# Prompt attention of a two-layer decoder: 64-row score products in two halves, five score banks, two rows of lead

## The chip, the cores and the metric

The kernel runs on one core of a Trainium2 chip. TensorE (PE) multiplies into PSUM banks, VectorE (DVE) and ScalarE (ACT) evict and transform, GpSimd (POOL) is a third elementwise engine, and SyncE (SP) issues the DMAs. The metric is the device time of one launch in microseconds, the median of several runs.

## The reference

One inference step of a two-layer decoder for a prompt of 2048 rows and a sample group of 64 rows: a gated linear attention layer, then a differential attention layer. The part in question is the prompt's differential attention, with 8 heads of 128 values, each in two halves m = 0, 1 of 64:

```python
s = jnp.einsum('bqhmd,bkhmd->bhmqk', qs, ks).astype(F32) * (DIFF_DH ** -0.5)   # DIFF_DH = 64
s = s + bias[None, :, None]                       # bias by distance, constant from a distance of 128 on
s = jnp.where(rel >= 0, s, jnp.finfo(F32).min)    # causal
p = jax.nn.softmax(s, axis=-1)
a = p[:, :, 0] - lam * p[:, :, 1]
return jnp.einsum('bhqk,bkhd->bqhd', a, v.astype(F32))
```

## The kernel before

The program is a sequence of stages with a barrier between them: projection, recurrence, residual, projection, prompt attention, sample attention, residual. The change touches the prompt attention alone.

It goes over 8 heads H, and in each over 16 query rows i, a row being a tile of 128 queries against its (i+1)*128 keys. The keys of a row are cut into pieces of at most 512 columns from the right (10 at 1, 4 at 4 pieces: 40 pieces a head for each half m). A loop of three rounds covers two heads each; heads 6 and 7 stand behind it.

- **Scores** (`scores`, L1609 and L1610). Operands are split into a high and a low float32r part, so that three partial products are needed for q times k (high-high, high-low, low-high). `q_hl` holds for each half m the 64 rows of the high part of q over the 64 rows of its low part, and `k_hi`, `k_lo` hold each half's keys twice, one copy over the other. So one product over 128 rows gives two partial products at once, and a piece takes two of them, into one of four banks `ps_s`.
- **Preparation** (`prep`, `high`, `low`). The q and k of the next head are loaded (`load_nat`, 8 DMAs for each of four groups of rows), turned by TensorE four tiles at a time (L1590) into the bank `ps_k`, copied as the high part by ACT (L1680) and subtracted as the low part by DVE (L1739 for q, L1742 for k). There are 16 such steps for a head, one beside each row.
- **Eviction** (`take`, L1765 and L1773). DVE adds the bias, writes the scores of the row to `s_sb` and keeps the maximum of each piece. Behind the last piece it reduces the maxima (L1780) and negates them (L1782).
- **Exponentials** (`exps`, L1686). ACT raises both halves of the row and sums them (`total`). `take` and `exps` run one row ahead of the rest.
- **Combination** (`combine`, L1790 to L1798). DVE takes the reciprocal of the two sums, the weight of the second half, and writes `a` = first half + weight * second half.
- **Turning and values** (`turn` L1623, `copies` L1698, `meet` L1637, `output` L1705). TensorE turns `a` in groups of four tiles into two banks `ps_a`, ACT copies them to `a_t` (two buffers), TensorE multiplies them by v in full float32 (two records for each tile), ACT scales the row and SP stores it.

TensorE's order is written out by hand: for row i the preparation step, then the scores of row i+2 with the turning and the values of row i mixed in from the fourth score piece on. DVE's order in `head` is `take(i+1)`, `combine(i)`, `low`. Each engine works strictly in its own order and waits on semaphores.

## Time and profile before

| | |
|---|---|
| median of 3 runs | 4059.39 us (4054.75 to 4062.89) |
| the profiled execution | 4064.68 us, its span 4062.9 us |
| PE busy | 3668.9 us (90%), 19279 products |
| DVE busy | 1798.8 us (44%) |
| ACT busy | 1123.8 us (28%) |
| POOL busy | 118.7 us (3%) |
| mean granted TensorE clock | 0.953 of full speed |

The shares are means over all stages. The prompt attention has about 900 us of the span, from its first DMA at 2257 us to its last output at 3154 us, and it is the only long stretch in which DVE is busy for more than eight tenths of the time. A busy PE in the profile includes the tail of each product, so the spacing of starts says more than the busy time.

### The profile page before, as it was taken

The numbers are of one execution on the slowest core, as the hardware profiler recorded it, in microseconds if no ns is written. First come the engines' busy times: TensorE is split into PE (matmuls) and PEld (weight loads), VectorE is DVE, ScalarE is ACT, GpSimd is POOL, SyncE is SP. The second block draws the span as 40 slices with busy tenths as digits, with TensorE's granted clock in tenths as the row PEclk, the third lists the DMA queues.
The fourth block names the chain that finished last, engine by engine and source line by source line (L and its number), as shares of the span: only waits on it lengthen the run. The fifth ranks groups of instructions, "written<-read, shape, count | busy, mean of one in ns | idle before, by whom it ended". The sixth has DMA issues, their size and how long they took to land. (4 is left out here: it accounts for less than half of the span.)

```text
span 4062.9 us, 56102 instructions
## 1 busy us (share of the span) xinstructions
PE 3668.9 (90%) x19279; PEld 3005.8 (74%) x19279; DVE 1798.8 (44%) x4077; ACT 1123.8 (28%) x1848; POOL 118.7 (3%) x156
## 2 busy tenths in 40 slices
PE   3999997995999989999999688888888799779999
PEld 2788896774788868888888577777777677458887
DVE  2122201555555542223000588888888222165554
ACT  1111101332221221112000366666666111121111
POOL 0000001110000000000000000000000000000000
PEclk7999998998999989999999799999999899889999
DMA  5433443336222244334222622222210555242221
GB/s 141 146 125 106 142 138 119 114 105 226 74 88 83 73 164 145 108 124 146 98 98 90 132 64 64 54 52 54 64 33 12 200 200 205 104 157 85 74 85 47
DMA packets 321076, 440.41 MB, mean 108 GB/s; under 512 B 155213, under 2 KB 214382, under 8 KB 320894
## 3 DMA queue, kind: packets, MB, share of 16 engines
q1 hardware_dynamic: 320894, 438.24, 33.2%
q8 instruction: 83, 1.36, 0.1%
q14 instruction: 99, 0.81, 0.1%
HBM read 296.46 MB, written 141.70 MB: 108 GB/s over the span
## 5 line engine op out<-in xcount | busy, mean ns | idle before, releaser
L318 PE MATMUL in_ps_y<-in_w_hi,in_x_hi 128*128 128x512 f32 (+2 forms) x2040 | 771.6, 378 | 12.8 <-ACT in_w_hi L359 5.5
L320 PE MATMUL in_ps_y<-in_w_lo,in_x_hi 128*128 128x512 f32 (+2 forms) x2040 | 768.4, 377 | 0.0
L322 PE MATMUL in_ps_y<-in_w_hi,in_x_lo 128*128 128x512 f32 (+2 forms) x2040 | 768.3, 377 | 0.0
L318 PEld LDWEIGHTS in_ps_y<-in_w_hi,in_x_hi 128*128 128x128 f32 x2040 | 385.0, 189 | 76.9 <-issue 11.7
L322 PEld LDWEIGHTS in_ps_y<-in_w_hi,in_x_lo 128*128 128x128 f32 x2040 | 384.7, 189 | 64.2
L320 PEld LDWEIGHTS in_ps_y<-in_w_lo,in_x_hi 128*128 128x128 f32 x2040 | 384.9, 189 | 63.1
L1637 PE MATMUL att_ps_o<-att_v,att_a_t 128*128 128x128 f32 x2176 | 296.2, 285 | 55.3 <-ACT att_a_t L1698 54.7
L1637 PEld LDWEIGHTS att_ps_o<-att_v,att_a_t 128*128 128x128 f32 x2176 | 277.8, 197 | 80.6 <-ACT att_a_t L1698 56.8
L1765 DVE TENSOR_SCALAR_CACHE_REDUCE att_s<-att_ps_s,att_far 128x512 f32<-128x512 f32 (+3 forms) x608 | 326.7, 582 | 6.0 <-PE att_ps_s L1610 2.0
L439 DVE COPY in_out<-in_ps_y 128x512 f32<-128x512 f32 (+1 forms) x85 | 55.8, 657 | 604.8 <-PE in_ps_y L322 604.8
L1686 ACT ACTIVATE att_s<-att_s,att_neg 128x128 f32<-128x128 f32 (+15 forms) x256 | 307.1, 1200 | 2.7 <-DVE att_neg L1782 2.1
L1609 PE MATMUL att_ps_s<-att_k_hi,att_q_hl 128*128 128x512 f32 (+3 forms) x640 | 260.9, 414 | 11.7 <-DVE att_s L1765 10.8
L372 ACT ACTIVATE in_out<-in_ps_y 128x512 f32<-128x512 f32 (+1 forms) x102 | 56.3, 552 | 740.2 <-PE in_ps_y L322 663.2
L1610 PE MATMUL att_ps_s<-att_k_lo,att_q_hl 128*128 128x512 f32 (+3 forms) x640 | 235.5, 373 | 0.0
L1202 PE MATMUL res_ps_f<-res_w_hi,res_o_hi 128*128 128x512 f32 x544 | 220.7, 406 | 7.8 <-ACT res_w_hi L1314 3.9
L1202 PE MATMUL res_ps_g<-res_w_hi,res_h_hi 128*128 128x512 f32 x544 | 219.2, 403 | 3.9 <-issue 3.9
L1204 PE MATMUL res_ps_f<-res_w_lo,res_o_hi 128*128 128x512 f32 x544 | 217.3, 399 | 0.0
L1206 PE MATMUL res_ps_f<-res_w_hi,res_o_lo 128*128 128x512 f32 x544 | 216.9, 399 | 0.0
L1206 PE MATMUL res_ps_g<-res_w_hi,res_h_lo 128*128 128x512 f32 x544 | 216.5, 398 | 0.0
L1204 PE MATMUL res_ps_g<-res_w_lo,res_h_hi 128*128 128x512 f32 x544 | 216.4, 398 | 0.0
L1623 PE MATMUL att_ps_a<-ident,att_a 128*128 128x128 f32 x1088 | 162.4, 279 | 35.0 <-DVE att_a L1798 33.6
L1698 ACT ACTIVATE att_a_t<-att_ps_a 128x512 f32<-128x512 f32 (+2 forms) x320 | 159.7, 531 | 120.9 <-PE att_ps_a L1623 119.9
(242 smaller groups left out, 5078.4 us busy)
## 6 DMA issues: line engine op xcount, KB each, us to landing
smp_k_pg<-in_cache_k SPq DMA_DIRECT2D x64, 512.0 KB, 5.1
smp_v_pg<-in_cache_v SPq DMA_DIRECT2D x64, 512.0 KB
x_turned<-in_x_hi SPq DMA_DIRECT2D x34, 512.0 KB, 5.0
x_turned<-in_x_lo SPq DMA_DIRECT2D x34, 512.0 KB, 5.8
factors<-in_out SPq DMA_DIRECT2D x68, 256.0 KB, 2.0
in_x_hi<-x_turned SPq DMA_DIRECT2D x34, 512.0 KB, 4.3
in_x_lo<-x_turned SPq DMA_DIRECT2D x34, 512.0 KB, 5.1
res_factors<-factors SPq DMA_DIRECT2D x34, 512.0 KB
```

What stands on the lines that cost most here:

```text
L318: nc.tensor.matmul(ps_y[g][:, cols], x_hi[u][:, k, :], w_hi[g][:, k, cols], start=(k == 0), stop=False)
L320: nc.tensor.matmul(ps_y[g][:, cols], x_hi[u][:, k, :], w_lo[g][:, k, cols], start=False, stop=False)
L322: mm = nc.tensor.matmul(ps_y[g][:, cols], x_lo[u][:, k, :], w_hi[g][:, k, cols], start=False, stop=(k == KD - 1))
L1202: nc.tensor.matmul(dst[:, cols], hi[kind][:, k, :], w_hi[n][:, k, cols], start=(k == 0), stop=False)
L1204: nc.tensor.matmul(dst[:, cols], hi[kind][:, k, :], w_lo[n][:, k, cols], start=False, stop=False)
L1206: mm = nc.tensor.matmul(dst[:, cols], lo[kind][:, k, :], w_hi[n][:, k, cols], start=False, stop=(k == K - 1))
L1609: nc.tensor.matmul(dst, lhs, k_hi[u][m][:, lo_:hi_], start=True, stop=False)
L1610: nc.tensor.matmul(dst, lhs, k_lo[u][m][:, lo_:hi_], start=False, stop=True).then_inc(s["piece_ready"], 1)
L1623: mm = nc.tensor.transpose(ps_a[n % 2][:, (b % 4) * P:(b % 4 + 1) * P], a[i % 2][:, b * P:(b + 1) * P], core.ident[:, :])
L1637: mm = nc.tensor.matmul(ps_o[:, 0:D_VD], a_t[n % 2][:, (b % 4) * P:(b % 4 + 1) * P], v_sb[u][:, b, :], start=(b == 0), stop=(b == i))
L1686: nc.scalar.activation(s_sb[i % 2][:, m, 0:n], s_sb[i % 2][:, m, 0:n], ACT.Exp, bias=neg[i % 2][:, m:m + 1], accum_out=total[i % 2][:, m:m ...
L1765: ins = nc.vector.tensor_scalar(s_sb[i % 2][:, m, lo_:cut], ps_s[n % RING][:, 0:cut - lo_], far[u][:, :], None, ALU.add, ALU.max, accum_ou ...
```

## The change

The scores are computed with products over 64 rows. Half m lies on rows 64m to 64m+63 of `q_hi`, `q_lo`, `k_hi`, `k_lo`, each kept once, and a pair of pieces (the same keys for m = 0 and 1) takes six products: high-high, high-low, low-high, each for m = 0 on the upper 64 rows and m = 1 on the lower 64, into two banks. There are five banks `ps_s` in place of four and no `ps_k`; the preparation shares the two `ps_a`. The preparation has 8 steps for a head in place of 16 and `load_nat` 2 DMAs for each group in place of 8.

All scores are kept with the opposite sign (`HEAD_SCALE` is negative, the bias comes from `rev_neg`), so that the row's minimum is what ACT needs; it is one `tensor_reduce` right behind the row's evictions. `take` and `exps` run two rows ahead (`LAG`), TensorE's scores three rows and two pairs (`LEAD`). `s_sb` has four buffers, `a_t` eight. The reciprocal and the weight are computed on GpSimd with three small operations. The values of row i are multiplied in the iteration behind that in which it is turned.

```diff
+    HEAD_SCALE = -(D_DH ** -0.5)
+    SLOTS, ROW_RING, TURN_RING = 5, 4, 8
+    LAG, LEAD = 2, 2
...
+    prep_at = {1: 0, 3: 1, 5: 2, 7: 3, 9: 4, 11: 5, 13: 6, 14: 7}
...
-        q_hl = [[sb(f"q_hl{u}{m}", [P, SEQ], F32R) for m in range(2)] for u in range(2)]
-        s_sb = [sb(f"s{i}", [P, 2, SEQ]) for i in range(2)]
+        k_hi = [sb(f"k_hi{u}", [P, SEQ], F32R) for u in range(2)]
+        k_lo = [sb(f"k_lo{u}", [P, SEQ], F32R) for u in range(2)]
+        q_hi = [sb(f"q_hi{u}", [P, SEQ], F32R) for u in range(2)]
+        q_lo = [sb(f"q_lo{u}", [P, SEQ], F32R) for u in range(2)]
...
-        ps_k = ps("ps_k")
...
-                        for side in range(2):
-                            for m in range(2):
-                                sp.dma_start(nat[:, 4 * g:4 * g + 4, m, side, :],
-                                             src[g * BANK:(g + 1) * BANK, bass.ds(h * D_VD + m * D_DH, D_DH)]
-                                             .rearrange("(t p) d -> p t d", p=P)).then_inc(nat_in[g], 16)
+                        sp.dma_start(nat[:, 4 * g:4 * g + 4, :],
+                                     src[g * BANK:(g + 1) * BANK, bass.ds(h * D_VD, D_VD)]
+                                     .rearrange("(t p) d -> p t d", p=P)).then_inc(nat_in[g], 16)
...
+                    pe.wait_ge(s["piece_free"], after(PIECES * H + 2 * at + 2))
+                    for q_part, k_part in ((q_hi, k_hi), (q_hi, k_lo), (q_lo, k_hi)):
+                        for m in range(2):
+                            rows = slice(m * D_DH, (m + 1) * D_DH)
+                            mm = nc.tensor.matmul(ps_s[(2 * at + m) % SLOTS][:, 0:hi_ - lo_],
+                                                  q_part[u][rows, i * P:(i + 1) * P], k_part[u][rows, lo_:hi_],
+                                                  start=(q_part is q_hi and k_part is k_hi), stop=(q_part is q_lo))
+                    mm.then_inc(s["piece_ready"], 1)
...
+                    for i in range(1, T + 1):
+                        turning = [] if last and i == T else list(range(groups[i % T]))
+                        end = PAIRS if last else 2 * PAIRS
+                        row = i + LAG + 1
+                        filling = [n for n in range(first_pair(row) + LEAD, first_pair(row + 1) + LEAD) if n < end]
+                        meeting = list(range(groups[i - 1]))
+                        for step in range(max(len(turning), len(filling), len(meeting) + 1)):
+                            if step < len(turning):
+                                turn(H, u, i, step, last)
+                            if step == 0 and i in prep_at and not last:
+                                prep(H + 1, prep_at[i], bank_free(H, last, ("prep", i, prep_at[i])))
+                            if step < len(filling):
+                                scores(H, u, filling[step])
+                            if step >= 1 and step - 1 < len(meeting):
+                                meet(H, u, i - 1, step - 1)
...
+                    for i in range(1, T + 1):
+                        turning = not (last and i == T)
+                        more = not (last and i + LAG >= T)
+                        if turning:
+                            copies(H, u, i, 0, 1, last)
+                            if not last and i in prep_at:
+                                use = bank_uses(last).index(("prep", i, prep_at[i]))
+                                high(H + 1, 1 - u, prep_at[i], ps_a[use % 2])
+                        if more:
+                            exps(*ahead(H, u, i, LAG), 0)
+                        if turning:
+                            copies(H, u, i, 1, 3, last)
+                        if more:
+                            exps(*ahead(H, u, i, LAG), 1)
+                        if turning:
+                            copies(H, u, i, 3, 4, last)
+                        output(H, i - 1)
...
+                def weights(H, i):
+                    r = i % ROW_RING
+                    pool.wait_ge(s["exp_done"], after(2 * (T * H + i + 1 + ROW_RING)))
+                    nc.gpsimd.tensor_tensor(inv[r][:, :], total[r][:, :], minus_one[:, :],
+                                            ALU.pow).then_inc(s["inv_done"], 1)
+                    pool.wait_ge(s["inv_done"], after(T * H + i + 1))
+                    nc.gpsimd.tensor_tensor(ratio[:, :], total[r][:, 0:1], inv[r][:, 1:2],
+                                            ALU.mult).then_inc(s["ratio_done"], 1)
+                    pool.wait_ge(s["ratio_done"], after(T * H + i + 1))
+                    nc.gpsimd.tensor_tensor(weight[r][:, :], ratio[:, :], core.neg_lambda[:, :],
+                                            ALU.mult).then_inc(s["weight_done"], 1)
...
+                        for m in range(2):
+                            bank, at = ps_s[(2 * n + m) % SLOTS], col
                             if cut > lo_:
-                                ins = nc.vector.tensor_scalar(s_sb[i % 2][:, m, lo_:cut],
-                                                              ps_s[n % RING][:, 0:cut - lo_], far[u][:, :], None,
-                                                              ALU.add, ALU.max, accum_out=mx[:, m, col:col + 1])
-                                col += 1
+                                ins = nc.vector.tensor_scalar(s_sb[r][:, m, lo_:cut], bank[:, 0:cut - lo_],
+                                                              far[u][:, :], None, ALU.subtract, ALU.min,
+                                                              accum_out=low_of[i % 2][:, m, at:at + 1])
+                                at += 1
...
+                def lowest(H, u, i, cols):
+                    dve.wait_ge(s["piece_free"], after(PIECES * H + 2 * first_pair(i + 1) + SLOTS))
+                    dve.wait_ge(s["exp_done"], after(2 * (T * H + i + 1)))
+                    nc.vector.tensor_reduce(shift[i % ROW_RING][:, :], low_of[i % 2][:, :, 0:cols], AX.X,
+                                            ALU.min).then_inc(s["shift_done"], 1)
...
-                    dve.wait_ge(s["exp_done"], after(2 * (T * H + i + 1)))
-                    if i >= 2:
-                        dve.wait_ge(s["o_copied"], after(T * H + i - 1))
-                    nc.vector.reciprocal(inv[i % 2][:, :], total[i % 2][:, :]).then_inc(s["inv_done"], 1)
-                    dve.wait_ge(s["inv_done"], after(T * H + i + 1))
-                    nc.vector.scalar_tensor_tensor(weight[:, :], total[i % 2][:, 0:1], core.neg_lambda[:, :],
-                                                   inv[i % 2][:, 1:2], ALU.mult, ALU.mult).then_inc(s["weight_done"], 1)
...
-                        if not (last and i + 1 >= T):
-                            take(*ahead(H, u, i, 1))
+                        more = not (last and i + LAG >= T)
+                        if more:
+                            lowest(*ahead(H, u, i, LAG), take(*ahead(H, u, i, LAG)))
+                        if not last and i - 1 in prep_at:
+                            n = prep_at[i - 1]
+                            use = bank_uses(last).index(("prep", i - 1, n))
+                            low(H + 1, 1 - u, n, ps_a[use % 2])
                         combine(H, u, i)
```

## Rows read from the trace of the kernel before

**Rows 1.** Busy time by window, attention: stretch, length, PE, PEld, DVE, ACT, POOL, clock, DMA.
```profile
2257.00:2287.10 30.10, 14.04 (x72) 12.08 (x72) 13.40 (x30) 10.22 (x20) 0.00 (x0) 0.61 1.13 213
2287.10:2400.70 113.60, 96.39 (x618) 81.84 (x619) 93.75 (x313) 71.47 (x135) 0.00 (x0) 0.92 0.38 76
2400.70:2509.30 108.60, 95.88 (x646) 81.77 (x645) 93.81 (x313) 73.09 (x137) 0.00 (x0) 0.98 0.25 61
...
2951.20:3058.00 106.80, 94.91 (x635) 81.20 (x634) 92.52 (x312) 72.65 (x137) 0.00 (x0) 0.97 0.13 32
3058.00:3154.10 96.10, 85.40 (x576) 73.76 (x574) 80.41 (x282) 63.81 (x118) 0.00 (x0) 0.98 0.04 12
```

**Rows 2.** Who waited for whom, 2287 to 3154 us: total, times, longest.
```profile
ACT att_o L1705 <- DMA mixer_out<-att_o: 32.4, 7, 8.1
DVE att_q_hl L1739 <- ACT att_q_hl L1680: 27.9, 15, 6.4
DVE att_inv L1790 <- ACT att_s L1686: 25.3, 12, 3.8
DVE att_k_lo L1742 <- ACT att_k_hi L1680: 22.0, 8, 4.4
```

**Rows 3.** Groups of instructions by form, attention: count, busy us, mean ns, idle before.
```profile
L1637 PE MATMUL att_ps_o<-att_v,att_a_t 128*128 128x128 f32 x2176 | 296.2, 285 | 55.3 <-ACT att_a_t L1698 54.7
...
L1609 PE MATMUL att_ps_s<-att_k_hi,att_q_hl 128*128 128x512 f32 x448 | 197.4, 441 | 10.3 <-DVE att_s L1765 9.6
...
L1623 PE MATMUL att_ps_a<-ident,att_a 128*128 128x128 f32 x1088 | 162.4, 279 | 35.0 <-DVE att_a L1798 33.6
```

**Rows 4.** Timeline of TensorE, around row 13 of head 3: start, length, instruction.
```profile
2705.30 0.47 PE L1609 MATMUL att_ps_s<-att_k_hi,att_q_hl 128*128 128x512 f32 x1
2705.61 0.39 PE L1610 MATMUL att_ps_s<-att_k_lo,att_q_hl 128*128 128x512 f32 x1
2705.84 0.39 PE L1609 MATMUL att_ps_s<-att_k_hi,att_q_hl 128*128 128x512 f32 x1
...
2712.19 1.06 PE L1637 MATMUL att_ps_o<-att_v,att_a_t 128*128 128x128 f32 x8
2713.08 0.38 PE L1623 MATMUL att_ps_a<-ident,att_a 128*128 128x128 f32 x2
```

**Rows 5.** Timeline of TensorE in the sample attention: 8-row products among 128-row ones.
```profile
3240.97 1.07 PE L2042 MATMUL smp_ps_o<-smp_v_new,smp_a_new 8*64 8x512 f32 x2
3241.96 7.08 PE L2040 MATMUL smp_ps_o<-smp_v_pg,smp_a_t 128*64 128x512 f32 x16
3248.97 1.07 PE L2042 MATMUL smp_ps_o<-smp_v_new,smp_a_new 8*64 8x512 f32 x2
```

**Rows 6.** Timeline of DVE behind the evictions of a row and in the next, head 3.
```profile
2704.11 0.16 DVE L1780 TENSOR_REDUCE att_top<-att_mx 128x2 f32<-128x10 f32 x1
2704.31 0.17 DVE L1782 TENSOR_SCALAR att_neg<-att_top 128x2 f32<-128x2 f32 x1
...
2705.03 2.08 DVE L1798 SCALAR_TENSOR_TENSOR att_a<-att_s,att_weight 128x1792 f32<-128x1792 f32 x1
2707.15 0.69 DVE L1739 SCALAR_TENSOR_TENSOR att_q_hl<-att_ps_k,att_q_hl 64x512 fp32r<-64x512 f32 x1
...
2709.22 0.75 DVE L1765 TENSOR_SCALAR_CACHE_REDUCE att_s<-att_ps_s,att_far 128x512 f32<-128x512 f32 x1
...
2709.89 0.48 DVE L1765 TENSOR_SCALAR_CACHE_REDUCE att_s<-att_ps_s,att_far 128x256 f32<-128x256 f32 x1
```

**Rows 7.** Groups of instructions, GpSimd over the whole span.
```profile
L1338 POOL TENSOR_TENSOR res_rstd<-res_rstd,minus_half 128x1 f32<-128x1 f32 x34 | 18.7, 551 | 418.9 <-DVE res_rstd L1386 418.9
```

**Rows 8.** Timeline of the attention's start: DMA issues of SP, then DVE's first eviction.
```profile
2256.99 3.39 SPq L1537 DMA_DIRECT2D att_k_nat<-out_k  x4
...
2276.24 0.54 SPq L1542 DMA_DIRECT2D att_v<-out_v  x1
...
2284.11 0.29 DVE L1773 CUSTOM_DVE_ANT_0 att_s<-att_ps_s,att_bias 128x128 f32<-128x128 f32 x1 [0.37 <-DMA att_far<-in_rel_bias]
```

More of the change, by code:

```diff
@@ new lines, in bank_free @@
+                def bank_free(H, last, use):
+                    order = bank_uses(last)
+                    at = order.index(use)
+                    kind, i, n = order[at - 2] if at >= 2 else ("prob", 0, at - 2)
+                    if kind == "prep":
+                        pe.wait_ge(s["lo_done"], after(PREPS * (H + 1) + n + 1))
+                    else:
+                        done = GROUPS * (i // T) + first_group[i % T] + n + 1
+                        pe.wait_ge(s["a_copied"], after(GROUPS * H + done + 2))
+                    return ps_a[at % 2]
@@ new lines, in turn @@
+                def turn(H, u, i, g, last):
+                    H2, u2, i2 = ahead(H, u, i)
+                    if g == 0:
+                        pe.wait_ge(s["a_done"], after(T * H2 + i2 + 1 + ROW_RING))
+                    bank = bank_free(H, last, ("prob", i, g))
+                    for b in range(4 * g, min(4 * g + 4, i2 + 1)):
+                        mm = nc.tensor.transpose(bank[:, (b % 4) * P:(b % 4 + 1) * P],
+                                                 a[i2 % 2][:, b * P:(b + 1) * P], core.ident[:, :])
@@ L1673, in _ @@
+                pe.sem_inc(s["a_met"], TURN_RING)
+                pe.sem_inc(s["a_turned"], groups[T - 1])
+                for n in range(PREPS):
+                    prep(0, n, first_banks[n])
+                for n in range(first_pair(LAG + 1) + LEAD):
+                    scores(0, 0, n)
+                turn(0, 0, 0, 0, False)
+                for n in range(first_pair(LAG + 1) + LEAD, first_pair(LAG + 2) + LEAD):
+                    scores(0, 0, n)
                 over_heads(pe, head)
@@ L1708, in head @@
                 def head(H, u, last):
-                    for i in range(T):
-                        todo = [] if last else list(enumerate(slots(i)[0]))
-                        for n, (is_q, m, g) in todo[:1]:
-                            high(H + 1, 1 - u, slots(i)[1] + n, is_q, m, g)
-                        more = not (last and i + 1 >= T)
-                        if more:
-                            exps(*ahead(H, u, i, 1), 0)
-                        copies(H, i, 0, 2)
-                        if more:
-                            exps(*ahead(H, u, i, 1), 1)
-                        copies(H, i, 2, groups[i])
-                        output(H, i)
-                        for n, (is_q, m, g) in todo[1:]:
-                            high(H + 1, 1 - u, slots(i)[1] + n, is_q, m, g)
@@ L1777, in take @@
-                                col += 1
+                                    out=s_sb[r][:, m, start:hi_], in0=bank[:, start - lo_:hi_ - lo_],
+                                    in1=bias[u][:, NEAR - (n_keys - start):NEAR], scale=1.0, scalar=3.0e38,
+                                    op0=ALU.add, op1=ALU.min, accum_out=low_of[i % 2][:, m, at:at + 1])
+                                at += 1
                             ins.then_inc(s["piece_free"], 1)
-                    dve.wait_ge(s["piece_free"], after(PIECES * H + first_piece[i + 1] + RING))
@@ L1814, in _ @@
+                        combine(H, u, i)
+                for n in range(PREPS):
+                    low(0, 0, n, first_banks[n])
+                dve.wait_ge(s["lo_done"], after(PREPS))
+                dve.sem_inc(s["piece_free"], SLOTS)
+                dve.sem_inc(s["a_done"], ROW_RING)
+                dve.sem_inc(s["shift_done"], 2)
+                for i in range(LAG):
+                    lowest(0, 0, i, take(0, 0, i))
                 over_heads(dve, head)
```

278 lines of the change are left out of this document (124 added, 154 removed).

## The prediction

> **What bounds the kernel now.** I read the busy time by window first, because the page's shares are means over seven stages. From the first to the last instruction of the prompt attention [rows 1] there are 30 us of start, seven heads that take 110.1 us each ((3058.0 - 2287.1) / 7) and an eighth of 96.1 us. In a head DVE is busy for 93.7 us and PE's records cover about 96, but these overlap: a product of 512 columns is recorded with 0.39 us and the next one starts 0.23 us behind it [rows 4]. By spacing PE needs less. With 0.111 us for each 128-column record (0.89 us for 8, rows 4), the values take 2176 / 8 x 0.111 = 30.2 us, the turning 1088 / 8 x 0.111 = 15.1 us [rows 3], the preparation 64 x 0.111 = 7.1 us. Of the 160 score products of a head 112 are 512 wide (448 in all for each of the two lines, rows 3), 25.8 us at 0.23; the 48 narrower ones lie between 0.11 and 0.17 us by their width, some 6.5 us. Together 84.7 us, so DVE is the fuller engine.
>
> The waits say where the other 16 us of a head go. DVE waited 27.9 + 22.0 us for high parts of the preparation and 25.3 us for exponentials [rows 2], together 9.4 us a head. The cause of much of it is at the head's start, where ACT's `output` stood for a store (32.4 us in seven waits, rows 2) and everything behind it on ACT with it; at the head's end `take` of the short row 0 is done at once and `combine(15)` waits for two long exponentials. Behind row 5 DVE hardly waits: the timeline behind a row's evictions is one dependent instruction after the other [rows 6].
>
> **DVE's part.** Today 0.92 us pass from the start of the reduction to that of the combination (2704.11 to 2705.03, rows 6). The negation, the reciprocal and the weight go away; the reduction (0.16 us) stays, with some 0.05 us to the next start. This gives back 0.7 us a row, 11.2 us a head. The preparation has 8 steps fewer at 0.69 us (rows 6; the low part of q is 64x512 there, and the k part of 128 rows costs the same 0.69, so the full-height q part should too): 5.5 us. The evictions and the combination stay as they are. A subtract or a minimum in the place of an add or a maximum is not in the trace; I take the same duration, since only the operation changes. DVE's work falls from 93.7 to 77 us, 81 with the short gaps between dependent instructions.
>
> **TensorE's part.** Preparation: 32 records fewer, 3.6 us. Turning and values stay, 45.3 us. The scores go from two products a piece and half to three, so for a pair of pieces from four to six. No row here shows two 64-row products on different halves of the array. The bounds: if the two of a step run at once, a step costs what one product costs, 0.23 us at 512 columns, and for narrow pieces not less than two weight loads of 0.11 us. That is 28 pairs x 3 x 0.23 + 12 x 3 x 0.22 = 27.2 us a head, against 32.3 now. If they run one after the other it is 28 x 6 x 0.23 + 12 x 6 x 0.135 = 48.4 us. These ends are far apart. I take the lower one: the nearest row is the 128-row product [rows 4], which streams all 128 rows in the same 0.23 us, and two 64-row products together read no more rows and load no more cells.
>
> The Trainium skill supports this: TensorE: Matmul & The Clock Gate, in Part 3 on packing small matmuls, says that products on distinct row groups run concurrently, with starts some 4 ns apart. No row of this trace shows it. The other way, TensorEngine Tiling (Array Packing), Key Properties, says that a change of the tiling mode drains the engine. By that rule every pair of this kernel pays a drain on both sides, since its neighbours use all 128 rows.
>
> What a visit to another shape costs can be seen: the two 8-row products of the sample attention take 0.99 us to the next start, where two of their 128-row neighbours take 7.01 / 16 x 2 = 0.88 [rows 5], so 0.11 us a visit. The first float32r product behind float32 ones has 0.31 us to the next start, and not 0.23 [rows 4], 0.08 more. There are 40 visits a head, one a pair: 40 x 0.19 = 7.6 us. (Today's visits are fewer, as the scores often stand in runs.) PE: 45.3 + 3.5 + 27.2 + 7.6 = 83.6 us. So PE hardly gets shorter, while DVE does, and PE becomes the fuller engine by a little.
>
> **Waits and queues.** GpSimd takes the reciprocal and the weight. Its power on 128x1 took 0.55 us [rows 7]; on 128x2 I take 0.7, the two products between 0.15 and 0.55 each, so a chain of 1.0 to 1.8 us. It starts when the exponentials of row i end, and `combine(i)` comes a whole `take` and `combine` later, at least 2 us on short rows and 7 on long ones, so it is hidden; without that cover it would cost up to 1 us on rows 0 to 3. GpSimd has nothing else queued here. `lowest` adds a wait for exponentials four rows back, long past. With two rows of lead the wait for exponentials at row 15 goes too (25.3 / 8 = 3.2 us a head). At a head's start SP now issues 2 DMAs before v and the bias and not 8; at 0.54 us each (2.16 for four, and 3.39 for the first four with their start, rows 8) this is 3.2 us sooner for the stores for which ACT stood. What is late next is TensorE's third turning group at rows 9 and 11: its bank waits for the low part of a preparation step, which DVE does only behind the next `take`. At row 9 that is 13 tiles x 2 x 0.67 / 4 = 4.4 us of evictions (0.67 us for four tiles, rows 6), 0.2 of reduction and 0.7 of low part, 5.3 us behind the combination, where TensorE is there after two groups turned, the preparation, two pairs and a group of values, 2 x 0.44 + 0.44 + 2 x 0.88 + 0.89 = 4.0. Behind it are the score pairs of the next row; DVE has two pairs in hand, so I take 1 us for each.
>
> Over 83.6 us of PE I set 5 us for what doesn't overlap (these two, short rows, the loop's turn). A head: 88.5 us.
>
> **The start and the end.** v is issued at 2276.2 behind 32 DMAs, DVE's first eviction is 7.9 us later [rows 8]. Now 8 DMAs stand before it; with 8 preparation steps, each in a bank of its own, it comes some 15 us sooner, and I take 13, for two rows are to be evicted before the exponentials matter. Head 7 loses 11.2 us of DVE work and its row-15 wait: 82 us for 96.1.
>
> **Sum.** 7 x (110.1 - 88.5) = 151, and 14 and 13: 178 us. The profiled execution is 4064.7 us, 1.8 outside its span and 5 above the median of the runs; I take the 178 from the median: 4059 - 178 = 3881 us.
>
> **The rivals.**
> - *DVE sets the pace* (0.17): the visits cost nothing and PE stays under 80 us. The head is 82 us, DVE's work and gaps: 197 + 14 + 13 = 224 less, 3835 us. For it: float32 turning and values are already switched with float32r scores today. Against: rows 5.
> - *PE and DVE take turns* (0.20). Only 2.5 pairs fit in five banks, and TensorE can't turn row i before the combination. Where one engine has a long iteration, the other's is short: at row 13 DVE evicts row 15 and combines, 5.4 + 0.2 + 0.7 + 2.1 = 8.4 us, and PE has 14 tiles to turn, the one pair of row 0, 13 tiles of values and the preparation, 5.8 us; a row later DVE has 3.7 and PE 6.1. If neither can run ahead, the larger counts in each; over the 16 rows that is 92 us, with 4 for the short rows and the loop 96: 99 + 9 + 13 = 121 less, 3938 us.
> - *The halves don't overlap* (0.12): PE needs 83.6 + 21.2 = 104.8 us, with 4.5 not hidden 109.3. The heads gain 6 us in all, the start 13 and the end nothing: 4040 us.
> - *The halves exclude each other* (0.05), the one on the other side: the product on one half starts only when that on the other has left the array, so each takes its recorded 0.39 us and not 0.23 (rows 4; 0.27 for narrow ones). The scores then cost 28 x 6 x 0.39 + 12 x 6 x 0.27 = 85 us a head, PE 141, the head 146: 7 x 36 + 25 more, 4320 us. It decides from 112 us a head on, that is, if a 64-row product costs over 0.015 us more than a full one with no overlap.
> - *As forecast* (0.46): 85 to 92 us a head, 3857 to 3906 us.
>
> **Range and chances.** 3815 to 3965 us holds the first three cases, with bounds of the unknown terms, and leaves out the two without overlap. A difference of 0.2% (8 us) is about what a measurement of this kernel can tell from none. Faster 0.91 (the case without overlap mostly belongs here), within 0.2% 0.03, slower 0.06.
>
> **What would show it.** In the profile after: pairs of score records that start within a few hundredths of a microsecond, the next step 0.23 us behind; if starts are 0.23 us apart within a pair, the third rival holds. DVE busy 77 us a head. Heads of 88 us. Few waits of DVE for exponentials or high parts; a wait of TensorE for `lo_done` at rows 9 and 11. DVE's first eviction near 2270 us. The prediction is wrong if the visits cost several tenths, if the granted clock falls in the attention (it is 0.92 to 0.98 in the heads now, rows 1), or if GpSimd's chain shows up before the combination.

## The result, and the profile after

The changed kernel takes 3945.5 us (median of 4 runs, 3944.4 to 3950.6), beside 4057.1 us for the kernel before on the same chip (4051.1 to 4062.9): a ratio of 0.9728, 95% interval 0.971 to 0.9745. That is 112 us less. 178 were forecast, and 3881 us; the range, 3815 to 3965 us, holds the result. One of the four executions of the kernel with the low part inside `take` (see the experiments) fell into a slower state of the chip (4681.7 us, mean granted clock 0.733) and is left out, so its median below is that of the other three.

The page's busy times, over all stages:

```profile
span 3943.8 us, 56028 instructions
PE 3622.2 (92%) x19663; PEld 2902.4 (74%) x19663; DVE 1679.3 (43%) x3629; ACT 1080.3 (27%) x1784; POOL 277.0 (7%) x541
```

The prompt attention by windows: the start, heads 0 to 6 together, heads 0 and 1, and most of head 7. The columns are start:end, length, then busy us and instructions of PE, weight load, DVE, ACT and POOL, the granted clock, the DMA share and GB/s.

```profile
2254.70:2273.30 18.60, 10.00 (x62) 8.00 (x62) 8.38 (x27) 6.54 (x16) 1.88 (x5) 0.68 0.98 264
2273.30:2944.40 671.10, 622.27 (x4678) 475.29 (x4677) 550.64 (x1792) 465.46 (x885) 137.93 (x335) 0.99 0.16 44
2273.30:2362.10 88.80, 81.88 (x599) 60.60 (x598) 78.60 (x256) 62.99 (x117) 19.07 (x47) 0.97 0.18 48
2362.10:2459.90 97.80, 91.37 (x686) 69.89 (x684) 78.82 (x257) 67.26 (x129) 19.59 (x48) 0.98 0.16 46
2944.40:3032.40 88.00, 85.43 (x662) 67.10 (x661) 70.47 (x229) 64.22 (x121) 18.33 (x45) 1.00 0.05 14
```

Against [rows 1] the start takes 18.6 us for 30.1. Heads 0 to 6 take (2944.4 - 2273.3) / 7 = 95.9 us each for 110.1, and head 7, from 2944.4 to 3038.5, takes 94.1 for 96.1. So the gain is 11.5 + 7 x 14.2 + 2 = 113 us. The forecast was 13 + 151 + 14. DVE's work fell as expected, to 78.7 us a head, but a head did not follow it down: neither engine is busy for all of it. The mean over seven heads hides the first one, which went from 113.6 to 88.8 us; heads 1 to 6 gained 12.5 us each.

The clock has a share in this. The seven heads of the kernel before, together:

```profile
2287.10:3058.00 770.90, 672.01 (x4411) 572.69 (x4412) 655.00 (x2184) 506.72 (x951) 0.00 (x0) 0.96 0.25 59
```

The granted clock rose from 0.96 to 0.99: 770.9 x 0.04 - 671.1 x 0.01 = 24 us of the heads' 99.8 would be the clock, if all of it came through. Head 0 alone went from 0.92 to 0.97. Whether the clock rose because of the change, no run here shows.

TensorE's timeline at rows 8 and 9 of a head. Columns: start, us, line, output<-inputs, tile shapes, count; a bracket is idle time before it and what ended it.

```profile
2602.17 0.28 PE L1624 MATMUL att_ps_s<-att_k_hi,att_q_lo 64*128 64x128 f32 x2
2602.37 1.16 PE L1662 MATMUL att_ps_o<-att_v,att_a_t 128*128 128x128 f32 x8
...
2605.79 0.65 PE L1648 MATMUL att_ps_a<-ident,att_a 128*128 128x128 f32 x4
2606.28 0.60 PE L1607 MATMUL att_ps_a<-ident,att_k_nat 128*128 128x128 f32 x4
2606.81 0.50 PE L1624 MATMUL att_ps_s<-att_k_hi,att_q_hi 64*128 64x512 f32 x2
2607.14 0.39 PE L1624 MATMUL att_ps_s<-att_k_lo,att_q_hi 64*128 64x512 f32 x2
2607.37 0.40 PE L1624 MATMUL att_ps_s<-att_k_hi,att_q_lo 64*128 64x512 f32 x2
2607.70 0.66 PE L1648 MATMUL att_ps_a<-ident,att_a 128*128 128x128 f32 x4
...
2611.87 0.44 PE L1648 MATMUL att_ps_a<-ident,att_a 128*128 128x128 f32 x2 [1.53 <-DVE att_k_lo L1794]
```

The two halves run at once: two products of 512 columns take 0.23 us to the next two (2607.14 to 2607.37), as long as one full-height product does in [rows 4]. But the visit costs more than what I took for it. The four products ahead of it take 0.53 us to the first score and not 0.44; the first step takes 0.33 and the last one 0.33, where 0.23 would do. Over the 117 visits with 512 columns between 2370 and 2940 us that stand free of waits, the mean is 0.14 us ahead of the scores and 0.19 in them, 0.33 a visit.

DVE behind the row's evictions, to be read beside [rows 6]:

```profile
2603.44 0.42 DVE L1826 CUSTOM_DVE_ANT_0 att_s<-att_ps_s,att_bias 128x256 f32<-128x256 f32 x1
2603.79 0.08 DVE L1826 DVE_READ_ACCUMULATOR2_ANT att_low_of<- 128x1 f32 x1
2604.00 0.16 DVE L1839 TENSOR_REDUCE att_shift<-att_low_of 128x2 f32<-128x8 f32 x1
2604.11 1.55 DVE L1848 SCALAR_TENSOR_TENSOR att_a<-att_s,att_weight 128x1280 f32<-128x1280 f32 x1
2605.57 0.35 DVE L1819 TENSOR_SCALAR_CACHE_REDUCE att_s<-att_ps_s,att_far 128x128 f32<-128x128 f32 x1
```

From the reduction to the combination it is 0.11 us and was 0.92. The reduction ends 0.05 us behind the combination's start: nothing that DVE does next waits for it.

The waits between 2273 and 3032 us (engine, tile and line that waited, what it waited for: us in all, times, the longest), to be read beside [rows 2]:

```profile
ACT att_o L1728 <- PE att_ps_o L1662: 114.7, 100, 3.0
ACT att_a_t L1720 <- PE att_ps_a L1648: 107.1, 124, 2.8
...
DVE att_k_lo L1794 <- ACT att_k_hi L1700: 36.5, 13, 5.8
DVE att_s L1819 <- PE att_ps_s L1624: 32.3, 59, 2.2
...
DVE att_a L1848 <- POOL att_weight L1777: 27.7, 10, 3.9
DVE att_q_lo L1791 <- ACT att_q_hi L1700: 19.5, 7, 2.9
...
PE att_ps_a L1648 <- DVE att_q_lo L1791: 10.6, 7, 1.5
PE att_ps_a L1648 <- DVE att_k_lo L1794: 10.6, 7, 1.5
...
ACT att_o L1728 <- DMA mixer_out<-att_o: 3.4, 3, 1.8
```

ACT's wait for a store fell from 32.4 to 3.4 us. DVE's wait for exponentials at row 15 is gone in heads 0 to 6, but exponentials are still waited for under another name: of the ten waits for the weight (27.7 us, beside 25.3 us for exponentials in [rows 2]) seven stand at row 1 of a head, 2.6 to 3.5 us each, and in each the weight's first operation starts 0.1 us behind the row's last exponentials, 1.3 us before the combination. DVE's wait for high parts is not gone either: 36.5 + 19.5 = 56.0 us, 8 a head, where [rows 2] have 49.9. Fourteen of these waits, 32 us, belong to the preparation steps of rows 13 and 14 (some 1.8 and 2.8 us each) and six, 24 us, to that of row 1: some 3.2 us in four heads, 5.8 and 5.5 us in heads 2 and 4, with which a round of the loop begins. DVE's timeline at the beginning of head 4:

```profile
2660.43 0.48 DVE L1848 SCALAR_TENSOR_TENSOR att_a<-att_s,att_weight 128x256 f32<-128x256 f32 x1 [2.57 <-POOL att_weight L1777]
...
2669.22 0.69 DVE L1794 TENSOR_TENSOR att_k_lo<-att_ps_a,att_k_hi 128x512 fp32r<-128x512 f32 x1 [5.45 <-ACT att_k_hi L1700]
```

TensorE works without a gap from 2651 to 2665.6 there, on the values of rows 14 and 15 with the turning of rows 15 and 0 and two score pairs between them; the preparation step of row 1, whose high part DVE waits for, stands behind them in TensorE's order. In heads 2 and 4 TensorE then stands for 1.7 and 1.9 us more, and the trace names nothing that it waited for. And TensorE in its turn waits 1.5 us for a low part in front of the third turning group of rows 9 and 11.

### The profile page after: what moved, and what is told of

Same layout as the page of the kernel before. It is cut to its first block and busy times, and to the rows that moved or that the text cites. A ratio compares the mean times of both kernels' runs of the same rounds, so it can differ in the third digit from the quotient of the medians.

```text
span 3943.8 us, 56028 instructions
## 1 busy us (share of the span) xinstructions
PE 3622.2 (92%) x19663; PEld 2902.4 (74%) x19663; DVE 1679.3 (43%) x3629; ACT 1080.3 (27%) x1784; POOL 277.0 (7%) x541
## 5 line engine op out<-in xcount | busy, mean ns | idle before, releaser
L1819 DVE TENSOR_SCALAR_CACHE_REDUCE att_s<-att_ps_s,att_far 128x256 f32<-128x256 f32 (+3 forms) x608 | 331.6, 581 | 35.3 <-PE att_ps_s L1624 32.3
L1662 PEld LDWEIGHTS att_ps_o<-att_v,att_a_t 128*128 128x128 f32 x2176 | 265.5, 192 | 61.6 <-issue 50.7
L1662 PE MATMUL att_ps_o<-att_v,att_a_t 128*128 128x128 f32 x2176 | 309.8, 286 | 0.5 <-ACT att_o L1728 0.5
L1707 ACT ACTIVATE att_s<-att_s,att_shift 128x128 f32<-128x128 f32 (+15 forms) x256 | 306.3, 1198 | 3.5 <-DVE att_shift L1839 3.5
L1648 PE MATMUL att_ps_a<-ident,att_a 128*128 128x128 f32 x1088 | 181.0, 282 | 39.9 <-DVE att_a L1848 13.1
L1720 ACT ACTIVATE att_a_t<-att_ps_a 128x512 f32<-128x512 f32 (+2 forms) x320 | 169.5, 533 | 111.4 <-PE att_ps_a L1648 107.9
L1848 DVE SCALAR_TENSOR_TENSOR att_a<-att_s,att_weight 128x128 f32<-128x128 f32 (+15 forms) x128 | 172.4, 1347 | 28.5 <-POOL att_weight L1777 27.7
L1648 PEld LDWEIGHTS att_ps_a<-ident,att_a 128*128 128x128 f32 x1088 | 122.0, 142 | 81.0 <-issue 37.7
```

The costliest lines, as they stand in the source:

```text
L1648: mm = nc.tensor.transpose(bank[:, (b % 4) * P:(b % 4 + 1) * P], a[i2 % 2][:, b * P:(b + 1) * P], core.ident[:, :])
L1662: mm = nc.tensor.matmul(ps_o[:, 0:D_VD], a_t[n % TURN_RING][:, (b % 4) * P:(b % 4 + 1) * P], v_sb[u][:, b, :], start=(b == 0), stop=(b == i))
L1707: nc.scalar.activation(s_sb[r][:, m, 0:n], s_sb[r][:, m, 0:n], ACT.Exp, bias=shift[r][:, m:m + 1], scale=-1.0, accum_out=total[r][:, m:m + ...
L1720: nc.scalar.activation(a_t[n % TURN_RING][:, 0:cols], bank[:, 0:cols], ACT.Copy).then_inc(s["a_copied"], 1)
L1819: ins = nc.vector.tensor_scalar(s_sb[r][:, m, lo_:cut], bank[:, 0:cut - lo_], far[u][:, :], None, ALU.subtract, ALU.min, accum_out=low_of[ ...
L1848: nc.vector.scalar_tensor_tensor(a[i % 2][:, 0:n], s_sb[r][:, 1, 0:n], weight[r][:, :], s_sb[r][:, 0, 0:n], ALU.mult, ALU.add).then_inc(s[ ...
```

## The experiments

They ran on three chips, each with the kernel before beside them (4058.8, 4056.5 and 4060.4 us). Ratios are to it. The changed kernel was not run again there, so the last column compares runs on different chips; worked out from the ratios, its entries differ by 1 to 7 us.

| kernel | median us | ratio (95%) | against the changed kernel |
|---|---|---|---|
| both halves on rows 0 to 63 | 4271.2 | 1.0513 (1.0492 to 1.0534) | +325.7 |
| four products of 128 rows | 3923.2 | 0.9669 (0.9653 to 0.9685) | -22.3 |
| scores two pairs at a time | 3964.5 | 0.9764 (0.9748 to 0.978) | +19.0 |
| low part inside `take` | 3911.4 | 0.9633 (0.9614 to 0.9653) | -34.1 |
| one row of lead | 4288.8 | 1.0567 (1.0549 to 1.0585) | +343.3 |
| weights on DVE | 3968.0 | 0.9775 (0.9759 to 0.9792) | +22.5 |
| two pairs, low part inside | 3916.7 | 0.9651 (0.9635 to 0.9667) | -28.9 |
| low part inside, preparation later | 3911.6 | 0.9639 (0.9622 to 0.9655) | -33.9 |
| TensorE 64 us more, rows 3 to 11 | 3993.1 | 0.9831 (0.9814 to 0.9847) | +47.6 |
| TensorE 64 us more, rows 13 to 15 | 4002.4 | 0.9856 (0.984 to 0.9873) | +56.9 |
| DVE 52 us more, rows 3 to 11 | 3987.1 | 0.9817 (0.9801 to 0.9834) | +41.6 |
| DVE 54 us more, rows 13 to 15 | 3971.4 | 0.9789 (0.9772 to 0.9805) | +25.9 |

To see where in a head the time goes, I took the starts of the combinations from DVE's timeline, and their distances from one row to the next, as a mean of heads 1 to 6 (us):

| kernel | head | rows 2 to 8 | rows 9 to 12 | rows 13 to 1 |
|---|---|---|---|---|
| before | 109.6 | 42.1 | 33.4 | 34.1 |
| changed | 97.0 | 33.9 | 34.1 | 29.1 |
| four products of 128 rows | 93.6 | 33.7 | 31.9 | 28.0 |
| scores two pairs at a time | 100.7 | 35.3 | 36.4 | 29.0 |
| low part inside `take` | 92.4 | 33.2 | 30.1 | 29.1 |
| one row of lead | 140.6 | 47.5 | 48.0 | 45.1 |
| weights on DVE | 100.1 | 37.3 | 33.8 | 29.0 |
| low part inside, preparation later | 92.3 | 37.4 | 30.1 | 24.8 |
| TensorE more, rows 3 to 11 | 102.8 | 36.3 | 37.5 | 29.0 |
| TensorE more, rows 13 to 15 | 104.4 | 33.9 | 34.4 | 36.1 |
| DVE more, rows 3 to 11 | 102.0 | 39.1 | 33.9 | 29.0 |
| DVE more, rows 13 to 15 | 100.3 | 33.9 | 36.4 | 30.0 |

These are heads of the one profiled execution of each kernel, with its clock. Row 2 stands for the distance from combination 2 to combination 3, and so on. The gain of the change is in rows 2 to 8 (8.2 us) and 13 to 1 (5.0); rows 9 to 12 gained nothing.

### Both halves on the same rows

```diff
-                            rows = slice(m * D_DH, (m + 1) * D_DH)
+                            rows = slice(0, D_DH)
```

> All six products of a pair lie on rows 0 to 63 (half 1 is computed from half 0's operands, so its values are not the reference's). Theory A, the two halves of the changed kernel overlap: the steps now take twice their time, 28 x 3 x 0.23 + 12 x 3 x 0.12 = 23.6 us more of TensorE a head; a head goes from 95.9 to 113 to 119 us and the time to 4080 to 4130 us. Theory B, they hardly overlap in the changed kernel: no change, 3945 us within 10.

It took 4271.2 us, far above what either theory gave. Two pieces of this kernel's timeline, the first at the full clock, the second at the half one:

```profile
2470.32 0.63 PE L1624 MATMUL att_ps_s<-att_k_lo,att_q_hi 64*128 64x512 f32 x2
2470.79 0.62 PE L1624 MATMUL att_ps_s<-att_k_hi,att_q_lo 64*128 64x512 f32 x2
...
2517.19 1.05 PE L1624 MATMUL att_ps_s<-att_k_lo,att_q_hi 64*128 64x512 f32 x2
2518.05 1.05 PE L1624 MATMUL att_ps_s<-att_k_hi,att_q_lo 64*128 64x512 f32 x2
```

On the same rows two products take 0.47 us, on different ones 0.23. That the halves overlap in the changed kernel is shown. A part of the loss is another thing, the clock. Two windows that follow on each other (columns as above):

```profile
2425.40:2490.00 64.60, 63.07 (x380) 49.66 (x378) 46.41 (x166) 37.97 (x80) 13.25 (x30) 1.00 0.19 55
2490.00:2542.00 52.00, 51.38 (x156) 37.58 (x157) 20.76 (x58) 16.97 (x25) 3.22 (x9) 0.51 0.02 5
```

The mean granted clock is 0.913 over a span of 4290.7 us, and 0.961 over 3943.8 us after the change: 4290.7 x 0.087 - 3943.8 x 0.039 = 219 us of the 347 that the span is longer would be the clock, if all of it came through. So the whole difference can't be read as the price of no overlap.

### Four products of 128 rows

```diff
-                    for q_part, k_part in ((q_hi, k_hi), (q_hi, k_lo), (q_lo, k_hi)):
+                    for q_part, k_part in ((q_hi, k_hi), (q_hi, k_lo)):
...
-                            rows = slice(m * D_DH, (m + 1) * D_DH)
+                            rows = slice(0, P)
...
-  stop=(q_part is q_lo))
+  stop=(k_part is k_lo))
```

> Four products over all 128 rows for a pair in place of six over 64 (the product of both halves, so values are not the reference's); as many products, rows and columns as the kernel before had, in the changed kernel's schedule. Theory A, a visit of the 64-row products costs 0.35 us against 0.1 for float32r products of full height: scores 32.2 + 40 x 0.1 = 36 against 24.6 + 40 x 0.35 = 38.6 us a head, so 2 to 3 us less a head, 3920 to 3935 us. Theory B, the price comes with any change of operands whatever the height: 7 us more a head, 4000 us.

22 us faster, though it streams four products a pair in turn. Its timeline:

```profile
2587.53 0.60 PE L1648 MATMUL att_ps_a<-ident,att_a 128*128 128x128 f32 x4
2587.88 0.71 PE L1624 MATMUL att_ps_s<-att_k_hi,att_q_hi 128*128 128x512 f32 x2
2588.43 0.63 PE L1624 MATMUL att_ps_s<-att_k_lo,att_q_hi 128*128 128x512 f32 x2
2588.90 1.05 PE L1662 MATMUL att_ps_o<-att_v,att_a_t 128*128 128x128 f32 x8
```

From the turning's start to the values' it is 1.37 us = 4 x 0.111 + 4 x 0.23: a visit of full height costs nothing. The record of the first float32r product starts early and is long, the turning's seems short, and the sum is right. So the 0.08 us that I read out of [rows 4] as part of a visit's price was none, and the whole 0.33 comes with the 64-row shape. The Trainium skill, TensorEngine Tiling (Array Packing), Key Properties, has a change of the tiling mode drain the engine; the traces agree as to where the time is lost, 0.33 us at a visit of 64-row products and none at one of full height. That it is the drain, and not another part of the switch, no run here shows.

With the spacings of these two traces a head's scores cost 28 x 3 x 0.235 + 12 x 3 x 0.135 = 24.6 us in halves, and 40 x 0.33 = 13.2 for the visits, 37.8 in all. In four products it is 28 x 4 x 0.235 + 12 x 4 x 0.135 = 32.8. The 64-row scores save no TensorE time: they cost 5.0 us a head more, of which 3.4 come through (with the clock's part: the heads of this run are at 1.00, those of the changed kernel at 0.99). What they give is that q and k are kept once, so that the preparation has half the steps.

### Scores two pairs at a time

```diff
-                            if step < len(filling):
-                                scores(H, u, filling[step])
+                            if step % 2 == 1:
+                                for n in filling[step - 1:step + 1]:
+                                    scores(H, u, n)
```

(Pairs left over follow behind the loop.)

> TensorE computes two score pairs at each second step where a row has them, 24 visits a head for 40. Theory A, the visits to the 64-row shape are what makes TensorE long: 16 x 0.35 = 5.6 us less a head, 45 in all, 3900 us. Theory B, five banks don't hold them: what is saved comes back as waits for free banks, 3940 us or more.

19 us slower, in rows 2 to 12. A visit with two pairs of 512 columns costs 0.32 us (median of 27), as much as one with a single pair, so fewer visits should have given TensorE some 5 us a head. Its waits:

```profile
ACT att_a_t L1724 <- PE att_ps_a L1648: 165.6, 148, 3.8
...
DVE att_s L1823 <- PE att_ps_s L1624: 65.0, 69, 2.3
```

These are 65.0 us and 165.6, where the changed kernel has 32.3 and 107.1. DVE gets its scores later, and TensorE stands in front of the turning for longer: 30.9 us for the combination and 30.3 for low parts, where the changed kernel has 13.1 and 21.2. That five banks are too few is not shown: TensorE's waits for a free bank are 8.1 us and were 6.8. A part of the profiled execution's loss is the clock (0.96 in heads 0 to 6, for 0.99).

### Low part inside take

```diff
-                            lowest(*ahead(H, u, i, LAG), take(*ahead(H, u, i, LAG)))
-                        if not last and i - 1 in prep_at:
-                            n = prep_at[i - 1]
-                            use = bank_uses(last).index(("prep", i - 1, n))
-                            low(H + 1, 1 - u, n, ps_a[use % 2])
+                            lowest(*ahead(H, u, i, LAG), take(*ahead(H, u, i, LAG), between))
...
+                        if between and c == min(1, len(pieces[i]) - 1):
+                            between()
```

(`between` holds the four lines taken out.)

> DVE computes the low part of a preparation behind the second pair of the row's evictions and not behind the last. Theory A, TensorE's wait for it at rows 9 and 11 lengthens the head: 22 us of waits go, 3925 us. Theory B, TensorE has slack there, or DVE then waits for ACT's high part: 3945 us within 8.

3911.4 us, 34 less than the changed kernel and more than the 21 us that its fourteen waits for low parts make, at 1.5 us each. Of its 4.6 us a head 4.0 are in rows 9 to 12. TensorE's waits for low parts are gone, and DVE's for scores, 32.3 us before the edit, are nearly so:

```profile
DVE att_s L1819 <- PE att_ps_s L1624: 5.3, 9, 2.0
```

That is what the short wait of TensorE had cost: the scores of the next row stood behind it in TensorE's order, and DVE behind them.

### Two pairs, low part inside

Both edits at once.

> Two score pairs a visit together with the low part behind the second pair. Theory A, the two-pair order lost only because turning and scores waited on the late low part: now 24 visits for 40 count, 3880 us. Theory B, it loses by itself, since DVE gets the pairs later: as much above 3912 us as the two-pair order was above the changed kernel, 3930 us.

3916.7 us, 5 us above the low part alone, which is about what can be told from none. The same edit cost 19 us on the changed kernel, so some three quarters of that loss came with the late low part. But neither theory's time came out: the 16 visits saved gain nothing even so. TensorE now waits for the combination in front of the turning, 25.6 us for 9.0 with the low part alone.

### Low part inside, preparation later

```diff
-    prep_at = {1: 0, 3: 1, 5: 2, 7: 3, 9: 4, 11: 5, 13: 6, 14: 7}
+    prep_at = {2: 0, 4: 1, 5: 2, 7: 3, 9: 4, 11: 5, 13: 6, 14: 7}
```

> The low part behind the second pair, and the first two preparation steps at rows 2 and 4 in place of 1 and 3. Theory A, at the head's turn DVE's wait for the first preparation delays combination and turning: 1 to 2 us a head less than with the low part moved alone, 3900 us. Theory B, TensorE is still at the values of row 15 then and sets the pace: 3912 us within 6.

No change (3911.6). Rows 13 to 1 fall from 29.1 to 24.8 us, and rows 2 to 8 rise from 33.2 to 37.4: the long distance at the head's turn moved by a row, with nothing gained. Theory B's time held. That whatever stands behind the values of rows 14 and 15 is late there, and not the preparation step as such, fits this; the run doesn't prove it.

### One row of lead

```diff
-    LAG, LEAD = 2, 2
+    LAG, LEAD = 1, 2
```

> The changed kernel with evictions and exponentials one row ahead in place of two, as in the kernel before (and TensorE's scores one row less ahead with them). Theory A, the second row hides the exponentials at the head's end and GpSimd's chain: without it DVE waits 3 to 8 us a head more, 3970 to 4010 us. Theory B, TensorE sets the pace and the second row gives nothing: 3945 us within 8.

343 us slower, far more than expected from the wait for exponentials. The waits of this kernel:

```profile
ACT att_a_t L1720 <- PE att_ps_a L1648: 429.4, 226, 4.3
DVE att_a L1848 <- POOL att_weight L1777: 401.0, 127, 8.5
...
PE att_ps_a L1648 <- DVE att_a L1848: 238.0, 112, 4.3
```

In ACT's new order the exponentials of row i+LAG stand behind the first copies of row i. With LAG 1 combination, turning, copy, exponentials, GpSimd's weight and the next combination are one chain. The waits fit this: DVE waits for the weight in front of 127 combinations. A part of the loss is again the clock: its mean is 0.934 over a span of 4286.2 us, so 4286.2 x 0.066 - 3943.8 x 0.039 = 129 us of the 343 would be the clock, if all of it came through. In any case the second row of lead is not an extra here: the order of ACT and the weight on GpSimd need it.

### Weights on DVE

The GpSimd block goes, and `combine` begins with

```diff
+                    dve.wait_ge(s["exp_done"], after(2 * (T * H + i + 1 + ROW_RING)))
+                    nc.vector.reciprocal(inv[r][:, :], total[r][:, :]).then_inc(s["inv_done"], 1)
+                    dve.wait_ge(s["inv_done"], after(T * H + i + 1))
+                    nc.vector.scalar_tensor_tensor(weight[r][:, :], total[r][:, 0:1], core.neg_lambda[:, :],
+                                                   inv[r][:, 1:2], ALU.mult, ALU.mult).then_inc(s["weight_done"], 1)
```

> The reciprocal and the weight back on DVE, behind the reduction as before; GpSimd does nothing in the attention. DVE's work rises by 0.5 us a row, 8.5 us a head. Theory A, TensorE sets the pace: less than 2 us a head, up to 3960 us; the waits for GpSimd's weight (27.7 us in ten) go. Theory B, DVE sets it: 8.5 us a head, 4010 us.

22.5 us slower, 2.8 a head, and by the table nearly all of it in rows 2 to 8 (33.9 to 37.3). In rows 9 to 15 the same DVE work is free. So the move to GpSimd is a fifth of the gain, and an addition of this size on DVE counts in rows 2 to 8 alone. The time lies between both theories.

### Work added to one engine

The test between "PE sets the pace", "DVE sets the pace" and "they take turns". TensorE turns its first group again (twice more at rows 3 to 11, or six times more at rows 13, 14 and 15):

```diff
-                    for b in range(4 * g, min(4 * g + 4, i2 + 1)):
+                    again = 2 if g == 0 and i in range(3, 12) else 0
+                    for b in (again + 1) * list(range(4 * g, min(4 * g + 4, i2 + 1))):
```

DVE combines 512 columns once more into a tile that nobody reads (once at rows 3 to 11, or three times at rows 13, 14 and 15):

```diff
+                        nc.vector.scalar_tensor_tensor(more_sb[:, :], s_sb[r][:, 1, 0:BANK], weight[r][:, :],
+                                                       s_sb[r][:, 0, 0:BANK], ALU.mult, ALU.add).then_inc(s["more"], 1)
```

> The changed kernel with TensorE work added and nothing else: at rows 3 to 11 the first group is turned twice more into the same bank, 8 records of 0.111 us a row, 8.0 us a head. Theory A, DVE and TensorE set the pace in turns, DVE at rows 2 to 12: under 4 us a head come through, 3945 to 3975 us. Theory B, TensorE sets the pace everywhere: 8 x 8.0, 4009 us.

> The same 8.0 us of TensorE a head, but at rows 13, 14 and 15. Theory A, TensorE sets the pace around the head's turn: all of it comes through, 8 x 8.0, 4009 us. Theory B, what is lost at the head's turn is waiting for DVE or for the loop: under 3970 us.

> DVE work added: at rows 3 to 11 one more combination of 512 columns into a tile that nobody reads, 0.7 us a row, 6.3 us a head. Theory A, DVE sets the pace there: 8 x 6.3, 3996 us. Theory B, TensorE sets the pace everywhere: 3960 us or less.

> The same 6.3 us of DVE a head at rows 13, 14 and 15. Theory A, DVE waits there anyway: under 2 us a head come through, up to 3960 us. Theory B, DVE's chain sets the head's turn: 3996 us.

The third one's group by form, which gives the size of DVE's addition (busy us, mean ns):

```profile
L1853 DVE SCALAR_TENSOR_TENSOR att_more<-att_s,att_weight 128x512 f32<-128x512 f32 x72 | 53.9, 748 | 1.3 <-issue 0.3
```

Starts are 0.67 us apart there and 0.78 in the fourth; from the instruction before to the combination it is 52 us more in all in the middle rows and 54 in the last. TensorE's 64 us added 47.6 us in the middle rows and 56.9 in the last; DVE's added 41.6 in the middle rows and 25.9 in the last. Two of the four times, 3993 and 3971 us, lie between both theories; the other two are near the first. If one engine set the pace, the other's addition would be free; in the middle rows the shares that come through are 0.74 and 0.80, in the last 0.89 and 0.48, and both pairs sum to well over 1, also with the 1 to 6 us less for each that the ratios give. By the distances in DVE's timeline TensorE's addition costs nothing at rows 3 and 4, then 0.7, 1.0, 1.4 and 0.9 us at rows 5, 7, 9 and 11, those with a preparation step, and 0.5, 0.1 and 1.1 us at rows 6, 8 and 10. DVE's costs 0.7 to 0.9 at each of rows 2 to 9 and nothing at rows 10 and 11. So no engine sets the pace throughout: which one's work counts changes from row to row, and in rows such as 7 and 9 that of both does. Whether they truly stand in turn there or are just equally long, these runs don't tell.

## Why the prediction was right, and where its sizes were off

The direction and the range were right, the case behind the forecast was not. The range had been drawn to hold three cases, and the time is near that of the second, to which I had given 0.20; that it lies in the range owes more to its width than to the forecast's mechanism.

**The heads.** 95.9 us where 88.5 were forecast, 7 x 7.4 = 52 us of the 65 that are missing.

- *The halves overlap* was right, and shown by taking the overlap away. The bound for narrow steps was too high: two products of 128 columns with their loads take 0.11 to 0.13 us a step (2602.05 to 2602.17), not 0.22. The scores cost 24.6 us, not 27.2.
- *The visits* are the first term that was mis-sized: 40 x 0.19 = 7.6 us, measured 40 x 0.33 = 13.2. The 0.11 came from 8-row products in another stage, the 0.08 from a record's start that costs nothing. TensorE's sum is then 30.2 + 15.1 + 3.6 + 24.6 + 13.2 = 86.7 us for 83.6: 7 x 3.1 = 22 us.
- *What doesn't overlap* is the second, 5 us a head, measured 95.9 - 86.7 = 9.2: 7 x 4.2 = 29 us. The place named for it was right (the wait for the low part at rows 9 and 11), its size was not. I set 1 us for each; it was 1.5, and what came of it 2 us each, for the early low part gives back 4.6 us a head, 4.0 of them in rows 9 to 12. I had argued that DVE's two pairs in hand would cover it. Up to 1 us a head of the 9.2 is the clock (671.1 x 0.01 over seven heads); the rest is a difference and was not taken apart further.
- *DVE's work* 78.7 us for 77. The terms held: low part 0.69 us at full height, subtract and minimum as long as add and maximum, reduction to combination 0.11 us.
- *The wait for the store*, 32.4 us to 3.4, and that for exponentials at row 15 went as forecast. What I did not see is that exponentials would be waited for at row 1 instead, with GpSimd's chain behind them: 22 us in seven waits. The waits for high parts, which were to become few, are 8 us a head. I had put them down to ACT standing for the store. In the new schedule the values come one iteration later, so TensorE has two long rows of them left when the head turns, and the preparation of row 1 is late for that (24 of the 56 us).

**Head 7** gained 2 us, not 14: I subtracted DVE's work and ACT's wait and did not follow the end. The last combination waits for its weight, because nothing stands between it and the last exponentials:

```profile
3025.16 2.35 DVE L1848 SCALAR_TENSOR_TENSOR att_a<-att_s,att_weight 128x2048 f32<-128x2048 f32 x1 [3.87 <-POOL att_weight L1777]
```

That wait is exponentials and the GpSimd chain together (the power starts at 3023.9, so the chain is 1.3 of the 3.9 us). DVE of the kernel before waited just as long there, for the exponentials alone (3.8 us, the longest such wait in [rows 2]). Behind the combination it takes 13.3 us to the end and took 9.6, as values of the last row come an iteration behind its turning.

**The start** gained 11.5 us for 13. DVE's first eviction is at 2269.6 (forecast: near 2270), 14.9 us behind the first DMA:

```profile
2269.59 0.29 DVE L1826 CUSTOM_DVE_ANT_0 att_s<-att_ps_s,att_bias 128x128 f32<-128x128 f32 x1 [1.78 <-DMA att_far<-in_rel_bias]
```

**GpSimd's chain** by form, beside [rows 7]:

```profile
L1771 POOL TENSOR_TENSOR att_inv<-att_total,att_minus_one 128x2 f32<-128x2 f32 x128 | 107.4, 839 | 592.2 <-ACT att_s L1707 592.2
L1774 POOL TENSOR_TENSOR att_ratio<-att_total,att_inv 128x1 f32<-128x1 f32 x128 | 26.3, 205 | 10.0
L1777 POOL TENSOR_TENSOR att_weight<-att_ratio,neg_lambda 128x1 f32<-128x1 f32 x128 | 24.3, 190 | 10.0
```

0.84 + 0.21 + 0.19 = 1.2 us, within 1.0 to 1.8. It is hidden as forecast, save where a head or the attention ends (27.7 us in ten waits, which hold the exponentials too).

**The rivals.** The time is near that of "PE and DVE take turns" (head 96, 3938 us), and the four runs with added work speak for its mechanism, the longer engine counting row by row. The forecast's case, a TensorE that sets the pace with little lost, fell. With the visits at their true price and no turns, a head would have been 86.7 + 5 = 91.7 us. "DVE sets the pace" fell too, except for rows 2 to 9, where its addition came through whole. No overlap and exclusion are refuted by the spacing. I had given the turns 0.20; the arithmetic there (92 us over the 16 rows) was as good as that of the forecast, and the choice between them rested on DVE's two pairs in hand. Two slips in the rivals change nothing here: 7 x 36 + 25 more is 4336 us, or 4323 with the start's 13 taken off, and not 4320; and 112 us a head stand for 0.011 us a product, not 0.015.

**What stays open.** Why the clock fell in the run with both halves on the same rows, and whether the change itself raised it in the heads. What part of the switch makes up the 0.33 us. What TensorE stands for when a round of the loop begins. Whether fewer visits would pay in another order: in the one that I tried, waits ate what they save.

**The best version** is the changed kernel with the low part inside `take`: 3911.4 us, 0.9% less than the changed kernel and 3.7% less than the kernel before.

## What to carry to other kernels

When two engines hand work back and forth through a few buffers, cost an iteration as the longer of both, row by row, before you sum each engine over the whole loop; and where a hand-off is late, price what stands behind the waiting instruction, since a wait of 1.5 us cost 2. Price a change of tile shape on the kernel's own alternation, from the start of the group before to the start of the group behind, for a single record's start can be early. A stage's last iteration is to be followed by itself: what lead and late values give in the loop, they take back at its end.

## What the runs showed of the hardware

- Two 64-row products on different halves of the array take the time of one, 0.23 us for 512 columns; for 128 columns both, loads and all, take 0.11 to 0.13 us.
- A visit to 64-row products among 128-row ones costs 0.33 us, with two pairs in it as with one (0.32); a visit of float32r products of full height among float32 ones costs nothing that the starts show.
- In the kernel with all 64-row products on rows 0 to 63 TensorE was granted 0.51 of its clock, the lower level of 1.2 GHz, for 52 us in which it was busy for 51.4. In the 64.6 us before, it had been busy for 63.1 at 1.00. There a step of two products took 0.86 us instead of 0.47. In the changed kernel, at as many products, the heads' windows are at 0.97 to 1.00.
- GpSimd's power on 128x2 took 0.70 us in the median, 0.84 in the mean and 1.63 at most; each product on 128x1 took 0.2 in the mean.
